# Two transformer layers on one core: weight remainders formed by accumulating transfers, and the first group of seven products prepared early

## What is computed

```python
a = rms_norm(h, attn_norm)
proj = a @ w_in                      # 1024 -> 3028 columns, for three head groups
o_a = dsa_attention(...)             # sparse attention, the top 128 keys by an indexer
o_b = forgetting_attention(...)      # softmax attention with a decay
o_c = gla_chunked(...)               # gated linear attention, chunks
h = h + concat(o_a, o_b, o_c) @ w_out
f = rms_norm(h, ffn_norm)
gate, up = split(f @ w_gate_up)
h = h + (silu(gate) * up) @ w_down
```

## Time and profile before

| | us |
|---|---|
| median of 3 runs | 1295.46 |
| the profiled execution, its own time | 1295.57 |
| its span in the profile | 1293.5 |
| PE busy | 1259.0 (97%) |
| PE weight loads busy | 1187.0 (92%) |
| DVE busy | 901.5 (70%) |
| ACT busy | 633.9 (49%) |
| POOL busy | 439.4 (34%) |
| POOL, the subtractions of L724, 116 of 2440 ns | 282.9 |
| mean share of the 16 DMA engines on the loads | 25% |

### The profile page before, as it was taken

The page is one execution under the profiler, slowest core; times in us unless marked ns, Lnnn a source line. Parts: engine busy times, 40 slices in busy tenths (PEclk is TensorE's granted clock), DMA queues, the critical chain, the costliest instruction groups (busy, mean ns, idle before and its releaser), DMA issues.

```text
span 1293.5 us, 22962 instructions
## 1 busy us (share of the span) xinstructions
PE 1259.0 (97%) x9174; PEld 1187.0 (92%) x9174; DVE 901.5 (70%) x1520; ACT 633.9 (49%) x1016; POOL 439.4 (34%) x230
## 2 busy tenths in 40 slices
PE   7999999998999999899999999999989999999998
PEld 7989999998999999899998889988779999997887
DVE  4598898488888888722236999984888888885110
ACT  5575556655444444522235665385464445454221
POOL 2563322143222222244445453122432222214543
PEclk9999999999999999999999999999999999999999
DMA  5312211033222231222223221110322332212333
GB/s 189 94 56 83 66 34 34 34 104 115 108 99 99 99 102 63 99 98 98 97 93 101 73 77 55 50 34 24 123 98 98 112 118 99 99 66 98 99 111 115
DMA packets 27440, 113.58 MB, mean 88 GB/s; under 512 B 3664, under 2 KB 4304, under 8 KB 21968
## 3 DMA queue, kind: packets, MB, share of 16 engines
q1 hardware_dynamic: 26624, 111.18, 25.2%
q10 hardware_dynamic: 720, 1.09, 0.2%
HBM read 108.79 MB, written 2.10 MB: 86 GB/s over the span
## 4 chain that ended last, share of the span: by engine, by line
PE 84%; DVE 9%; ACT 3%; issue 2%; DMA 1%; POOL 1%; SPq 0%; DVEq 0%; ACTq 0%; POOLq 0%
PE ps L1243 21%; PE ps L857 17%; PE ps L1249 11%; PE ps L863 8%; PE ps L954 5%; PE ps L960 5%; PE ps L955 5%; PE ps L1084 2%; PE ps L1057 1%; PE ps L1067 1%; PE ps L1032 1%; DVE rstd L2041 1%; DVE score L1866 1%; DMA raw<-in_groups 1%; PE ps L1141 1%
## 5 line engine op out<-in xcount | busy, mean ns | idle before, releaser
L724 POOL TENSOR_TENSOR wlo<-raw,whi 128x1024 fp32r<-128x1024 f32 x116 | 282.9, 2440 | 477.1 <-ACT whi L1327 476.6
L1327 ACT ACTIVATE whi<-raw 128x1024 fp32r<-128x1024 f32 x116 | 122.4, 1057 | 223.8 <-PE ps L863 179.1
L954 PE MATMUL ps<-xhi,whi 128*128 128x264 f32 (+1 forms) x632 | 177.6, 310 | 0.0
L955 PE MATMUL ps<-xlo,whi 128*128 128x264 f32 (+1 forms) x632 | 171.4, 300 | 0.0
L857 PE MATMUL ps<-hhi,whi 128*128 128x264 f32 (+1 forms) x528 | 159.0, 323 | 5.2 <-DVE hlo L2105 5.2
L857 PE MATMUL ps<-hlo,whi 128*128 128x264 f32 (+1 forms) x528 | 159.0, 323 | 0.0
L954 PEld LDWEIGHTS ps<-xhi,whi 128*128 128x128 f32 x632 | 119.1, 189 | 4.5 <-issue 0.4
L955 PEld LDWEIGHTS ps<-xlo,whi 128*128 128x128 f32 x632 | 119.2, 189 | 3.9
L857 PEld LDWEIGHTS ps<-hhi,whi 128*128 128x128 f32 x528 | 100.4, 190 | 13.5 <-DVE hlo L2105 5.8
L857 PEld LDWEIGHTS ps<-hlo,whi 128*128 128x128 f32 x528 | 100.2, 190 | 7.8
L829 POOL TENSOR_TENSOR sums_a<-raw 128x1024 f32<-128x1024 f32 x22 | 53.9, 2449 | 151.4 <-PE ps L1249 151.4
(11 more groups left out here) (275 smaller groups left out, 3337.8 us busy)
## 6 DMA issues: line engine op xcount, KB each, us to landing
raw<-in_weights SPq DMA_DIRECT2D x116, 512.0 KB, 3.3
raw<-in_groups SPq DMA_DIRECT2D x42, 1024.0 KB, 4.8
out_hT<-h SPq DMA_DIRECT2D x7, 256.0 KB, 4.5
h<-in_hT SPq DMA_DIRECT2D x4, 264.0 KB, 6.5
h<-in_hT ACTq DMA_DIRECT2D x4, 264.0 KB, 6.1
cst<-in_consts SPq DMA_DIRECT2D x1, 780.5 KB, 9.4
xnb<-feat SPq DMA_DIRECT2D x20, 33.2 KB, 2.0
feat<-xnb SPq DMA_DIRECT2D x20, 33.2 KB, 2.0
```

Source lines behind the costliest of these rows:

```text
L724: nc.gpsimd.tensor_tensor(wlo[:, b], raw[:, b], whi[:, b].bitcast(F32), ALU.subtract).then_inc(split_done, 1)
L954: nc.tensor.matmul(o, whi[:, k % 2, n], xhi[:, n, cut], start=(n == 0), stop=False)
L955: nc.tensor.matmul(o, whi[:, k % 2, n], xlo[:, n, cut], start=False, stop=False)
L1327: return nc.scalar.activation(whi[:, b], raw[:, b], ACT.Copy).then_inc(hi_done, 1)
```

## The change

For the 34 units of a layer ahead of the down projection, POOL subtracts no more. ACT writes `-whi` into `wlo` first (`negate_slot`) and rounds `whi` behind it; POOL then issues a DMA that reads the unit from HBM a second time and adds it to `wlo` in place (`add_unit`). The down projection keeps the subtraction. `raw` is free as soon as ACT is done with both. The load, the sums, the rounding and the remainders of group 1 move from behind the output projection into its last steps, and `prenorm(1)` on PE moves between the two low passes.

```diff
 
+        def added_to(l, n):
+
+            return added[n % 2], 16 * (l * (N_ADDED // 2) + n // 2 + 1)
+
+        def split_to(l, n):
+
+            return split_done, l * N_SPLIT + n - U_DN + 1
+
         def group_slot(n):
...
             def load_unit(n, b):
 
-                sp.wait_ge(split_done, n + 1)
+                if n >= 2:
+                    of, at = divmod(n - 2, UNITS)
+                    if at < U_DN:
+                        sp.wait_ge(hi_done, n - 1)
+                        sp.wait_ge(neg_done, of * N_ADDED + at + 1)
+                    else:
+                        sp.wait_ge(*split_to(of, at))
                 sp.dma_start(raw[:, b].rearrange("p k n -> p (k n)"), weights[n]).then_inc(raw_loaded[b], 16)
...
-                    load_unit(l * UNITS + n, n % 2)
-                for n in range(1, GROUPS_7 + 1):
+                def load_group(n):
+
                     if n == 1:
                         sp.wait_ge(ev.acc_free, 2 + 1)
                     elif n == 2:
@@ -696,6 +712,13 @@
                         sp.wait_ge(sv.group_lo, 3 * (g0 + n - 3) + 1)
                     sp.dma_start(group_slot(n)[0].rearrange("p b n -> p (b n)"),
                                  groups[l * GROUPS_7 + n - 1]).then_inc(sv.group_loaded[n % 2], 16)
+
+                for n in range(N_PROJ + 4, U_DN):
+                    load_unit(l * UNITS + n, n % 2)
+                    if n == U_OUT + 4:
+                        load_group(1)
+                for n in range(2, GROUPS_7 + 1):
...
-            pool.sem_inc(split_done, 2)
-
             def split_unit(n, b):
                 pool.wait_ge(hi_done, n + 1)
                 nc.gpsimd.tensor_tensor(wlo[:, b], raw[:, b], whi[:, b].bitcast(F32),
                                         ALU.subtract).then_inc(split_done, 1)
 
+            def add_unit(n):
+
+                of, at = divmod(n, UNITS)
+                pool.wait_ge(neg_done, of * N_ADDED + at + 1)
+                pool.dma_start(wlo[:, at % 2].rearrange("p k n -> p (k n)"), weights[n], accum_op=ALU.add).then_inc(added[at % 2], 16)
+
             for l in range(DEPTH):
...
+                zeroed, squared = [0], [0]
 
                 def proj(k, hf, p):
-                    split_unit(l * UNITS + k + 2, k % 2)
-                    split[0] += 1
+                    add_unit(l * UNITS + k + 2)
 
...
 
-                for n in range(N_PROJ + 2, U_DN):
-                    split_unit(l * UNITS + n, n % 2)
-
-                for n in range(1, GROUPS_7 + 1):
+                def pv_sums(n):
+
                     raw_blocks, _, sums, _, _ = group_slot(n)
                     pool.wait_ge(sv.group_loaded[n % 2], 16 * loads_before(l, n))
...
+                for n in range(N_PROJ + 2, U_DN):
+                    add_unit(l * UNITS + n)
+                    if n == U_OUT + 5:
+                        pv_sums(1)
+
+                for n in range(2, GROUPS_7 + 1):
+                    pv_sums(n)
+
+                for n in range(U_DN, UNITS):
                     split_unit(l * UNITS + n, n % 2)
+                if l < DEPTH - 1:
+                    for b in range(2):
+                        add_unit((l + 1) * UNITS + b)
 
 
...
                     if hf == 0:
-                        pe.wait_ge(split_done, l * UNITS + (n + 3))
+                        pe.wait_ge(*low_ready)
                     low_pass(n, b, bank_no, parts[hf], x, order, last).then_inc(half_done, 2 // len(parts))
...
-                prenorm(1)
                 for n in range(2):
-                    pe.wait_ge(split_done, l * UNITS + (U_GU + n + 3))
+                    pe.wait_ge(*added_to(l, U_GU + n))
                     for hf in range(len(parts)):
                         low_pass(n, n, 2 * n + hf, parts[hf], x_tiles, range(KT), True).then_inc(half_done, 2 // len(parts))
+                    if n == 0:
+                        prenorm(1)
...
+            def negate_slot(b):
+                nc.scalar.activation(wlo[:, b], raw[:, b], ACT.Copy, scale=-1.0).then_inc(neg_done, 1)
...
 
                     act.wait_ge(half_done, n * 2 + (half0 - 2))
                     act.wait_ge(raw_loaded[slot], (n - slot) * 8 + (raw0 + 16))
+                    if n % UNITS < U_DN:
+                        negate_slot(slot)
                     round_slot(slot)
...
                     elif m:
                         forms_high(m // 2 - 1)
+                    if m == 5:
+                        raw_high(1)
+                    elif m == 6:
+                        sums_high(1)
 
...
-                raw_high(1)
-                sums_high(1)
                 for n in range(1, GROUPS_7 + 1):
                     if n < GROUPS_7:
                         raw_high(n + 1)
...
                     elif m and m % 2 == 0:
                         forms_low(m // 2 - 1)
+                    if m == 5:
+                        rt_sums(1)
+                    elif m == 6:
+                        raw_low(1)
                 dve.wait_ge(ev.sum_hi, 1)
                 nc.vector.tensor_tensor(sum_parts[:, 1, of], rstd[:, of], sum_parts[:, 0, of].bitcast(F32), ALU.subtract).then_inc(ev.sum_split, 1)
                 forms(PAIRS - 1)
+                sums_low(1, SUM_P, 2)
                 forms_low(PAIRS - 1)
-
-                def rt_sums(n):
-
...
+                sums_low(1, SUM_R, 3)
```

More of the change, by code:

```diff
@@ L533, in hybrid_block @@
         hi_done = sem("hi_done")
+        neg_done = sem("neg_done")
+        added = [sem("added0"), sem("added1")]
         split_done = sem("split_done")
@@ L687, in _ @@
                     do[step[0]](*step[1:])
-                for n in range(N_PROJ + 4, U_DN):
-                    load_unit(l * UNITS + n, n % 2)
-                for n in range(1, GROUPS_7 + 1):
+                def load_group(n):
                     if n == 1:
@@ L865, in low_pass, with unit_part @@
                     return ins
-                def unit_part(b, n, bank_no, hf, parts, x, order=range(KT), first=True, last=True, waits={}):
+                def unit_part(b, n, low_ready, bank_no, hf, parts, x, order=range(KT), first=True, last=True, waits={}):
                     if hf == 0:
@@ L1168, in out @@
                         pe.wait_ge(hi_done, l * UNITS + (U_OUT + part + 1))
-                        pe.wait_ge(split_done, l * UNITS + (U_OUT + part + 3))
+                        pe.wait_ge(*added_to(l, U_OUT + part))
                         for n, hf in early:
@@ L1205, in _ @@
                         for hf in range(len(parts)):
[L1206 removed]
+                            unit_part(b, j * 2 + (U_OUT + b), (added[b], j * 16 + 16 * (l * (N_ADDED // 2) + U_OUT // 2 + 1)), 2 * b + hf, hf, parts, mix_tiles)
                 for ks in (range(KT - 1), (KT - 1,)):
@@ L2071, in sums_low @@
                                             ALU.subtract).then_inc(sv.group_lo, 1)
+                chain(nc.vector.memset(rstd[:], 0.0))
+                for m in range(KT):
+                    dve.wait_ge(half_done, half0 + 2 * (U_OUT + m + 1))
+                    nc.vector.tensor_tensor(tokens(l, h[:, m]), wide(l, 2 * (m % 2)), tokens(l, h[:, m]), ALU.add).then_inc(ev.acc_free, 1)
+                    dve.wait_ge(ev.acc_free, 2 + m + 1)
+                    x_low(m, par[:, P_FFN + m:P_FFN + m + 1], l * (2 * KT) + (KT + m), of)
+                    dve.wait_ge(ev.sq_ready, len(SQUARES) + m + 1)
+                    if m:
+                        dve.wait_ge(ev.summed, m)
+                    nc.vector.tensor_tensor(rstd[:, of], rstd[:, of], sqb[:, m % 2, of], ALU.add).then_inc(ev.summed, 1)
+                    if m % 2 and m < KT - 1:
+                        forms(m // 2)
+                    elif m and m % 2 == 0:
+                        forms_low(m // 2 - 1)
+                    if m == 5:
+                        rt_sums(1)
+                    elif m == 6:
+                        raw_low(1)
+                dve.wait_ge(ev.sum_hi, 1)
+                nc.vector.tensor_tensor(sum_parts[:, 1, of], rstd[:, of], sum_parts[:, 0, of].bitcast(F32), ALU.subtract).then_inc(ev.sum_split, 1)
+                forms(PAIRS - 1)
+                sums_low(1, SUM_P, 2)
+                forms_low(PAIRS - 1)
+                sums_low(1, SUM_R, 3)
                 def u_sum(n):
```

85 lines of the change are left out of this document (35 added, 50 removed).

## The result

| | before | changed |
|---|---|---|
| median, us | 1295.4 (4 runs) | 1329.99 (4 runs, 1329.78 to 1333.66) |
| span of the profiled execution, us | 1293.5 | 1328.1 |
| PE busy, us | 1259.0 | 1270.5 |
| PE idle, us | 34.5 | 57.6 |

The changed kernel is slower: the ratio is 1.0275, 95% interval 1.0257 to 1.0294, or 34.6 us. The prediction (1301.0, at most 1311) had the sign and not the size. PE executes the same 9174 matmuls, so the growth has two parts: 23.1 us of waits, and 11.5 us in which the same matmuls took longer.

The account below looks back on a forecast made before the run. PE was taken as the bound, busy 1259.0 of 1293.5 us, so new waits add almost in full. Seven terms summed to +5.5 us on the profiled 1295.57, giving 1301.0 us, range 1289 to 1311.

Parts of the forecast that it names:

- term 3: Mixers: PE waits for the later `wlo` at the tightest unit of each layer, 2.05 and 1.93 us, +4.0 us.
- term 4: Output projection, layer 0: PE waits for `wlo` at the first looped unit only, +1.2 us.
- terms 1 to 3: Start and mixers: ACT's first negations +0.5, waits removed by DVE's relief -3.3, waits added for `wlo` +4.0; together +1.2 us.
- Terms 6 and 7: Gate and up to group 1: third product later, low clock behind an idle stretch; +2.6 us layer 0, +1.1 layer 1.
- Term 5: Output projection, layer 1: later rounding and landing at the first looped unit, against 2.2 us of DVE waits removed; -0.6 us.
- Terms 1 and 2: ACT's negations of units 0 and 1 at the start, +0.5 us; mixer waits removed by DVE's relief, -3.3 us.
- the marks: Signs named beforehand, among them group 1's third product waiting 3 to 4 us on ACT's snapshot, clock about 0.5 behind it.
- B: Rival: DVE holds up POOL's issue of adding transfers, T 7.5 us, in mixers and output projections; 1316 us, chance 0.10.
- unit after unit: Sign that would show the forecast wrong by held-up transfers: PE waits for `wlo` at one unit after another.
- D: Rival: DVE isn't relieved, since the transfers' issue on POOL stops it as well; 1306 us, chance 0.05.
- A: Rival: adding transfers land early enough, T 3.3 us, no unit waits, clock stays up; 1292 us, chance 0.29.

Follow-up runs that it names:

- the second part alone: Kernel before with group 1 prepared early and the sum over the partitions between the two low passes, POOL still subtracting: 1309.7 us.
- POOL's late sums: POOL makes group 1's sums only after DVE's last sum is split: 1293.64 us on the kernel before, 1292.65 with 20 adding transfers, 1292.47 with 18.
- the run without transfers and second part: Changed kernel, POOL only raising the semaphore instead of 68 adding transfers, group 1 and the partition sum back in their old places: 1285.28 us.
- the two runs with 30 units: Kernel before with adding transfers for 30 mixer units: 1297.59 us; the same with the next load of the slot held until the landing: 1302.14 us.

## Why the prediction was wrong

**The step that failed is term 3** (mixers, waits added: +4.0), and term 4 with it: the time T of an adding transfer, and the count of the units that wait for it. PE waited 18.3 us for `wlo` in the mixers, and the stage of terms 1 to 3 grew by 22.1 us instead of 1.2.

- *T.* I took 5.5 us and measured is 7.0 from issue to landing, 7.3 from the end of the negation at unit 17. My estimate was 4.8 us for the addition counted as 1024 KB, plus up to 1.5 for sharing. Apart, the transfer takes 5.4 us; sharing adds 1.6; the issue on POOL starts 0.4 us behind the negation. The addition and the sharing are slightly above their bounds, the lag of the issue I had not counted, and inside those bounds I had taken 5.5. The rule of the Trainium skill that I set against the rows ("DMA: Bandwidth & Descriptors", section "Anatomy of one DMA") gave 4.4 us for the 1024 KB as which I counted it; an adding transfer took 5.4 us even apart, so the measurement decides against it for a transfer that adds.
- *Only the tightest unit counts.* I wrote that PE's wait at one unit gives the same time to the next, and so counted one unit per layer. PE waited at four in layer 0 and at nine in layer 1. ACT's negation stands in its list behind work that itself waits for PE: ahead of unit 17's, shown above, ACT had stood idle for 2.54 us until PE delivered. That a wait of PE so moves the next negations as well is argued from such rows; no run isolates it. The waits of layer 0's mixers fit "7.2 us less the room" unit by unit:

| unit | room before, us | wait after, us | sum |
|---|---|---|---|
| 3 | 6.54 | 0.93 | 7.5 |
| 9 | 5.00 | 2.24 | 7.2 |
| 11 | 5.25 | 2.09 | 7.3 |
| 17 | 3.45 | 3.46 | 6.9 |

Summed over all units with less room than 7.2 us, this gives 9.1 us for layer 0 (measured: 8.7) and 15.7 for layer 1 (measured: 9.6 for `wlo` and 2.2 for `xnb`). In layer 1 the sum is too high, since the room before is not the room that is left once POOL no longer subtracts. Its tightest unit, 14, had 3.57 us; in the run without transfers (timelines of ACT and PE):

```profile
754.57 1.06 ACT L1373 ACTIVATE wlo<-raw 128x1024 fp32r<-128x1024 f32 x1
...
761.65 1.14 PE L1002 MATMUL ps<-xhi,wlo 128*128 128x264 f32 x8
```

From the end of the negation (755.63) to the low pass are 6.02 us, and in the changed kernel PE waits only 0.98 us there. Counted with the room of this run, the sum is 11.8 us in layer 0 and 8.9 in layer 1, 20.7 against 18.3 measured. So my sentence was not all wrong: in this run units 10 and 12 of layer 0 have 6.2 and 6.0 us, too little, yet in the changed kernel they don't wait, and they stand right behind the waits at units 9 and 11. But units 9, 11 and 17 all wait. With my T of 5.5 and the room before, the sum of shortfalls would have given 7.7 instead of 4.0; with T = 7.2 and only the tightest units, 7.4. Neither correction alone comes near: the right T is what brings the many units with 5 to 7 us of room into play.

**The clock.** Terms 6 and 7 had the fall of the granted clock behind an idle stretch, terms 3 and 4 had not. In the mixers and in layer 0's output projection PE's busy time grew by 3.7 + 2.6 + 3.9 us (windows above), 10.2 of the 11.5 us. The stretches at 0.50 there are four: those of 3.4 us behind units 17 and 11 of layer 0, 6.8 us in the output projection, and 3.4 us in layer 1, behind the wait for `xnb`. By PE's busy time in them (15.8 us at half speed) they explain 7.9 us; where the other 2.3 come from is open. Not every wait was followed by a fall. Behind unit 11 (2.09 us of wait) and unit 9 (2.24 us):

```profile
100.60:104.00 3.40, 3.40 (x16) 0.50 0.62 102
...
85.00:95.00 10.00, 9.92 (x85) 1.00 0.48 107
```

**Term 4** (+1.2, measured +8.7): the first looped unit waited 3.43 us, PE then ran for some 5.5 us at half clock, and three later ones, with the 6.5 us that I had called enough, waited 0.3 to 0.7 us. **Term 5** (-0.6, measured +1.5): the waits for `h` went, as forecast, but PE waited for `wlo` twice, 2.15 and 1.05 us. **Terms 1 and 2** (-2.8) came out: without transfers the start and the mixers are 3.6 us shorter than before, 0.8 in layer 0 and 2.7 in layer 1. The 0.8 is no more than runs with untouched mixers show (0.7 us with the second part alone, 1.0 with POOL's late sums), so it may be chance.

**Terms 6 and 7** (+3.7, measured +2.4) look right, but that is luck: two errors cancel. DVE's relief alone shortens these stretches and what follows by 1.0 and 3.3 us (the run without transfers and second part), which I had left out; against that the second part costs 7.4 us, not 3.7. In layer 1 I also added 1.5 us for a low clock that the kernel before had already, behind its wait of 2.07 us (0.92 in its window above). Of the marks, the third product does wait for ACT's snapshot with a low clock behind it, but for 1.75 us in layer 0 and 3.33 in layer 1, where I had said 3 to 4.

**The rivals.** B came nearest, by its T of 7.5 us, its price of 1316 and its sign "unit after unit", but not by its mechanism: the issue on POOL took 0.88 us on average and 1.02 at most. Nothing in these runs shows DVE stopping it, and the same queue lands in 4.0 us without the addition. D is refuted: DVE's busy time fell from 901.5 to 841.5 us and the waits for it went. A's mechanism, few waits for `wlo`, holds for a transfer that does not add, but its price does not: at a landing of 4.0 us the time is 1298.2, not 1292. In that run's profile the stages of terms 6 and 7 grow by 4.8 us, where A had 0.65.

## What to carry to other kernels

When an operation that takes T is put between two steps of a pipeline, list the room of every unit and sum the shortfalls, not just the largest. Take the room from a run in which the change's other effects are already there: the sum with the room before was 24.8 us, with that of the run without transfers 20.7, measured 18.3. The largest shortfall of each layer alone gave 7.4. Count the room from the moment at which the issuing engine comes to the instruction, and use the slow way only for the units that have the room: here the same transfer cost 34.6 us on all 68 units (with the early group) and gained 1.6 us on 20 of them, 2.3 to 2.5 with POOL's late sums on top. Work that is moved "early" onto an engine has a price that depends on what else stops that engine there (11.4 to 14.5 us beside the subtractions, 7.4 without them); look at what runs beside it. And a wait that is put into the list of an engine which also issues small transfers holds those up as well.

## What the hardware showed

- An adding transfer of 512 KB from DRAM into SBUF lands in 5.4 us (median; shortest 5.1) when the next load of its slot is kept apart, and in 7.0 (up to 10.4) beside the loads; a plain one from the same queue, beside the loads, in 4.0. Its packets occupy the DMA engines 1.7 times as long (15.4% against 9.2%), and its issue on POOL takes 0.88 us against 0.54.
- Small transfers beside an adding one can be late: gathers of 33 KB, 2.0 us and at most 2.9 before, took up to 5.0 and 6.0 us in the two runs with 30 units.
- Behind PE's two waits of 3.4 us for `wlo` the granted clock stood at its lower level, 0.50, for 3.4 and 6.8 us, which by PE's busy time in them (3.4 and 5.6 us) cost 1.7 and 2.8 us on top. Behind waits of some 2 us it fell in one place (2.09 us) and stayed at 1.00 in another (2.24 us).
